# Second layer's temporaries packed by lifetime, expert pieces loaded into each slot as it comes free, a 17th slot, and the norm weights applied after the turn

## The reference

```python
for l in range(2):
    z = rms_norm(h, norm1_g[l]) @ w_in[l]
    y = concat(mlstm(..), mla(..), gla(..), conformer_conv(..))
    h = h + group_rms_norm(y, fuse_g[l], 4) @ w_out[l]
    u = rms_norm(h, norm2_g[l])            # h * rstd * norm2_g
    if l == 0: f = (silu(u @ w_gate) * (u @ w_up)) @ w_down     # dense, 2816 wide
    else:      f = moe_ffn(u, ...)         # 8 experts, each 1024 -> 2816 -> 1024
    h = h + f                              # moe: top 2 of 8 by u @ router, softmax of the two
return rms_norm(h, final_norm_g)
```

## Time and profile before

| | |
|---|---|
| median of 3 runs | 1104.01 us (1103.98 to 1105.52) |
| the profiled execution, its own time | 1104.98 us |
| its span, first to last instruction | 1103.1 us |
| granted TensorE clock | 0.998 of full |
| PE busy | 96% of the span |
| DVE, ACT, POOL busy | 28%, 28%, 23% |
| moved by DMA | 358.5 MB, mean 325 GB/s |
| first matmul of job 0 | at 430.58 us |
| expert jobs | 430.58 to about 1092 us |

### The profile page before, as it was taken

One profiled execution on the slowest core, in us unless ns is written; L12 is line 12 of the kernel. 1 busy time (PEld: TensorE's weight loads), 2 busy tenths in 40 slices (PEclk: granted clock), 3 DMA queues, 4 the chain that ended last, 5 costly groups with the idle time before them and its releaser, 6 DMA issues.

```text
span 1103.1 us, 27114 instructions
## 1 busy us (share of the span) xinstructions
PE 1063.6 (96%) x12186; PEld 766.0 (69%) x12186; DVE 305.1 (28%) x572; ACT 308.0 (28%) x571; POOL 251.0 (23%) x332
## 2 busy tenths in 40 slices
PE   7999999999999999999999999999989999999875
PEld 7888888888899887665656666766636766766531
DVE  4785644444558756110000010010000010010012
ACT  7868644434486871000000000000000000000011
POOL 9986300000078755400201002002001002001000
PEclk9999999999999999999999999999999999999999
DMA  9642995535424449999999999999999999999993
GB/s 302 208 158 78 391 351 188 169 139 151 134 68 167 163 167 419 411 417 390 416 420 416 419 418 417 419 419 418 418 421 417 419 419 419 419 419 419 420 418 156
DMA packets 81623, 358.50 MB, mean 325 GB/s; under 512 B 10108, under 2 KB 24654, under 8 KB 47840
## 3 DMA queue, kind: packets, MB, share of 16 engines
q1 hardware_dynamic: 76480, 344.15, 78.7%
q0 software_dynamic: 4848, 12.30, 3.2%
q10 hardware_dynamic: 176, 0.27, 0.1%
HBM read 350.35 MB, written 7.47 MB: 324 GB/s over the span
## 4 chain that ended last, share of the span: by engine, by line
PE 80%; DMA 8%; SPq 5%; ACT 3%; DVE 3%; issue 1%; DVEq 0%
PE bank L2718 25%; PE bank L2763 13%; PE bank L2730 5%; SPq L711 5%; PE bank L2194 4%; PE bank L2195 4%; PE bank L2196 4%; DMA ring<-in_moe_w_up_dram 3%; DMA low_raw<-in_moe_w_gate_dram 3%; DMA ring<-in_moe_w_down_dram 2%; PE bank L2770 2%; PE bank L2311 2%; PE bank L2313 2%; PE bank L2212 2%; PE bank L2213 2%; PE bank L2214 2%
## 5 line engine op out<-in xcount | busy, mean ns | idle before, releaser
L2718 PE MATMUL bank<-ring,spare 128*32 128x256 f32 x3028 | 181.1, 380 | 1.1 <-DMA ring<-in_moe_w_gate_dram 0.6
L2718 PEld LDWEIGHTS bank<-ring,spare 128*32 128x32 f32 x3028 | 120.2, 110 | 48.4 <-issue 8.3
L1057 ACT ACTIVATE high<-ring 128x2048 fp32r<-128x2048 f32 (+2 forms) x62 | 117.0, 1892 | 68.2 <-PE bank L2196 41.8
L830 POOL TENSOR_TENSOR low<-ring,high 128x512 fp32r<-128x512 f32 (+1 forms) x67 | 85.6, 1308 | 197.1 <-ACT high L1057 195.8
L1029 POOL DMA_INDIRECT expert_rows<-yrows,result_idx x15 | 15.1, 1004 | 397.0 <-ACT yrows L1428 394.0
L1525 DVE TENSOR_TENSOR low<-ring,high 128x2048 fp32r<-128x2048 f32 (+2 forms) x38 | 85.7, 2258 | 54.6 <-ACT high L1057 52.1
L2056 DVE TENSOR_TENSOR act_out<-bank,act_out 128x512 f32<-128x512 f32 (+3 forms) x37 | 20.5, 579 | 263.7 <-PE bank L2718 220.0
L2730 PE MATMUL bank<-ring,spare 128*64 128x256 f32 x700 | 86.4, 381 | 6.0 <-DMA ring<-in_moe_w_up_dram 6.0
L2763 PE MATMUL bank<-ring,hidT 128*32 128x256 f32 x1584 | 87.4, 379 | 0.0
L1446 ACT ACTIVATE hidT<-bank 128x512 f32<-128x512 f32 (+2 forms) x34 | 16.0, 536 | 231.9 <-PE bank L2743 231.9
L2044 DVE STREAM_TRANSPOSE spare<-back 128x768 f32<-128x768 f32 (+1 forms) x7 | 6.0, 861 | 250.9 <-DMA back<-token_rows,quad_idx 250.9
(11 more groups left out here) (478 smaller groups left out, 1772.4 us busy)
## 6 DMA issues: line engine op xcount, KB each, us to landing
ring<-in_moe_w_up_dram SPq DMA_DIRECT2D x72, 1024.0 KB, 27.6
ring<-in_moe_w_gate_dram SPq DMA_DIRECT2D x58, 1024.0 KB, 22.4
ring<-in_moe_w_down_dram SPq DMA_DIRECT2D x53, 1024.0 KB, 27.0
low_raw<-in_moe_w_down_dram SPq DMA_DIRECT2D x23, 1024.0 KB
ring<-in_w_in_dram SPq DMA_DIRECT2D x36, 512.0 KB, 5.7
raw_slots<-in_moe_w_gate_dram SPq DMA_DIRECT2D x15, 1024.0 KB
low_raw<-in_moe_w_gate_dram SPq DMA_DIRECT2D x15, 1024.0 KB
ring<-in_ffn_w_up_dram SPq DMA_DIRECT2D x22, 512.0 KB, 5.1
```

The lines of the kernel that those rows point to most:

```text
L830: last = pool.tensor_tensor(low[:, n % SPLIT, at], slot(n)[:, at], high[:, n % SPLIT, at].bitcast(F32), ALU.subtract)
L1057: act.activation(high[:, n % SPLIT, 0:width], slot(n)[:, 0:width], ACT.Copy).then_inc(s["high_ready"], 1)
L2718: last = pe.matmul(bank[b][32 * c:32 * c + 32, at:at + SEG], x[:, k, 32 * r:32 * r + 32], part, start=first and at == 0, stop=final and at ...
```

## The change

1. The second layer's temporaries in slots 5 to 10 are declared in an order by lifetime, so that they fill slots 5 to 8 only; short-lived ones share space (`gS`, `osq` over `qT`, `kT`; `dec`, `cqT` over `qtok`, `ktok`; `qksg` over `cumf` to `negm`; `probT` over `ckvT`, `rin`, `rt`). Eleven small tiles get space of their own. Slots 9 and 10 hold none.
2. `MOE_SLOTS` is reordered, and a slot that lay under temporaries waits for its own last readers (`SLOT_FREED`) and no longer for `mixers_done(1)`.
3. `un`, free after the attention's probabilities are turned, becomes a 17th slot `un_slot`: `DEEP = 17`, with piece 3 as its first.
4. `moe_g` and POOL's multiplication (L949) are gone. A small tile `gains` (feature p*8+k at partition p, column k) is loaded in layer 0 by one more DMA on POOL. PE reads h itself for L2653, with a step of 8 elements; POOL's L964 too. The norm weight is applied per partition when the turned tokens leave: for job 0 by four ACT activations with a scale and one DVE multiplication by a broadcast tile in place of two copies; for jobs 1 to 7 by one more DVE multiplication in place after the transpose.
5. `yrows` and `back` move over `u32`; job 0's tokens and the last squares go to `spare`.

```diff
-MOE_SLOTS = [4, 0, 1, 2, 3, 6, 7, 8, 9, 10, 5]
+MOE_SLOTS = [9, 10, 4, 5, 0, 8, 7, 1, 6, 2, 3]
-MOE_EARLY = 5
-DEEP = 16
+DEEP = 17
-RING_PLACE = [0, 1, 2, 3, 4, 5, 6, 7, 8, 9, 14, 15, 11, 12, 13, 10]
+RING_PLACE = [0, 1, 2, 16, 3, 4, 5, 6, 7, 8, 9, 14, 15, 10, 11, 12, 13]
+UN_AT = RING_PLACE.index(DEEP - 1)
+OVER_PLACES = [v for v in range(DEEP) if v != UN_AT][:RING]
@@ temporaries
             sb("ring_0_to_4", [P, 5, PIECE], F32, part)
-            (ckvT, cqT, moe_g, qtok, ktok, rin, rt, dec, gS, vm, gE, cumf, ... in a row)
+            with ExitStack() as first:
+                ckvT, rin, rt
+            probT, vm
+            with ExitStack() as scores:
+                qT, kT
+            gS, osq
+            with ExitStack() as tokens:
+                qtok, ktok
+            dec, cqT, gE, junk
+            with ExitStack() as gates:
+                cumf, aj, mrun, negm
+            qksg
@@ slots of the expert stage
+ [un_slot[:, :]]
+        SLOT_FREED = {5: (("pv_ready", DEPTH),),
+                      8: (("ga_ready", HEADS * DEPTH), ("qk_ready", DEPTH)),
+                      7: (("num_ready", DEPTH), ("y_c", DEPTH)),
+                      6: (("go_ready", DEPTH), ("y_g", DEPTH))}
@@ SP, expert()
                     elif RING_PLACE[g] < RING:
-                        if g == MOE_EARLY:
-                            sp.wait_ge(*mixers_done(1))
-                        elif MOE_SLOTS[RING_PLACE[g]] == 5:
-                            sp.wait_ge(s["hg_ready"], 2 * TT)
+                        for freed, count in SLOT_FREED.get(MOE_SLOTS[RING_PLACE[g]], ()):
+                            sp.wait_ge(s[freed], count)
                         sp.wait_ge(s["low_ready"], BEFORE_OF[MOE0 + RING_PLACE[g]] + 1)
                     elif RING_PLACE[g] < RING + SPLIT:
                         sp.wait_ge(s["piece_used"], MOE0 - SPLIT + RING_PLACE[g] - RING + 1)
-                    else:
-                        sp.wait_ge(*mixers_done(1))
+                    elif RING_PLACE[g] < RING + SPLIT + 2:
+                        sp.wait_ge(*mixers_done(1))
+                    else:
+                        sp.wait_ge(s["p_tr"], 3 * DEPTH)
@@ POOL
+                    pool.dma_start(gains[:, :], norm2_g[DEPTH - 1].rearrange("(p k) -> p k", p=P)).then_inc(s["moe_in"], 16)   # layer 0
-                if l:
-                    pool.wait_ge(s["qT_tr"], 4)
-                    pool.wait_ge(s["kT_tr"], 4)
-                    pool.dma_start(moe_g[:, :], bc(norm2_g[DEPTH - 1:DEPTH, :], [P, D])).then_inc(s["moe_in"], 16)
-            for t in range(TT):
-                for i in range(2):
-                    pool.wait_ge(s["h_ready"], 8 + 2 * t + i + 1)
-                    (un half t, i = h half * moe_g half, permuted).then_inc(s["hg_ready"], 1)
-                pool.wait_ge(s["hg_ready"], 2 * t + 2)
+                pool.wait_ge(s["h_ready"], 8 + 2 * t + 2)
-                feats = un[:, t, :].rearrange("p (b k q c) -> p b q k c", b=2, k=4, q=4)
+                feats = h[:, t, :].rearrange("p (q c b k) -> p b q k c", q=4, c=32, b=2)
@@ ACT
+            def x_out(x, n):
+                for k in range(4):
+                    last = act.activation(x[:, k, 0:n], bank[5][:, k * n:(k + 1) * n], ACT.Copy, scale=gains[:, k:k + 1])
+                last.then_inc(s["x_act"], 1)
@@ DVE
-                dve.transpose(x_of(n)..., xrows_q...).then_inc(s["xT_tr"], 1)
+                x = x_of(n)[:, :, 0:32 * r]
+                chain.done(dve.transpose(x..., xrows_q...))
+                chain.wait()
+                dve.tensor_tensor(x, x, bc(gains[:, :].unsqueeze(2), [P, KD, 32 * r]), ALU.mult).then_inc(s["xT_tr"], 1)
+            def x_out(x, n):
+                dve.tensor_tensor(x[:, 4:8, 0:n], bank[6][:, 0:4 * n].rearrange("p (k n) -> p k n", k=4),
+                                  bc(gains[:, 4:8].unsqueeze(2), [P, 4, n]), ALU.mult).then_inc(s["x_dve"], 1)
@@ PE
-            pe.wait_ge(s["hg_ready"], 2 * TT)
+            pe.wait_ge(s["h_ready"], 12)
+            by_k = h[:, :, :].rearrange("q t (p k) -> q t k p", k=KD)
-                        last = pe.matmul(bank[b][...], un[:, t, kd * P:(kd + 1) * P], sel[:, t, 0:96], ...)
+                        last = pe.matmul(bank[b][...], by_k[:, t, kd, :], sel[:, t, 0:96], ...)
```

More of the change, by code:

```diff
@@ L210, in build @@
             sb("ring_0_to_4", [P, 5, PIECE], F32, part)
[L211 to L222, removed]
-            vm = sb("vm", [P, TT, 256], F32, part)
[L224 to L241, removed]
+            with ExitStack() as first:
+                ckvT = sb("ckvT", [P, S], F32, first)
+                rin = sb("rin", [P, TT, 5, 32], F32, first)
+                rt = sb("rt", [P, 4, TT, 5, 16], F32, first)
+            probT = sb("probT", [P, 3, 4, P], F32, part)
+            vm = sb("vm", [P, TT, 256], F32, part)
             with ExitStack() as scores:
@@ L244, in build @@
                 kT = sb("kT", [96, 4, S], F32, scores)
-            probT = sb("probT", [P, 3, 4, P], F32, part)
+            gS = sb("gS", [P, 4, 3, P], F32, part)
             osq = sb("osq", [P, TT, 4, 64], F32, part)
+            with ExitStack() as tokens:
+                qtok = sb("qtok", [P, TT, 4, 96], F32, tokens)
+                ktok = sb("ktok", [P, TT, 4, 96], F32, tokens)
+            dec = sb("dec", [P, 4, 384], F32, part)
+            cqT = sb("cqT", [P, 2, S], F32, part)
+            ctok = cqT[:, :, :]
+            gE = sb("gE", [P, 5, P], F32, part)
+            junk = sb("junk", [P, 256], F32, part)
+            with ExitStack() as gates:
+                cumf = sb("cumf", [4, S], F32, gates)
+                aj = sb("aj", [4, S], F32, gates)
+                mrun = sb("mrun", [4, S], F32, gates)
+                negm = sb("negm", [P, S], F32R, gates)
+            qksg = sb("qksg", [P, 4, S], F32, part)
         with ExitStack() as part:
@@ L283, in build @@
         router = sb("router", [P, KD, E])
+        gains = sb("gains", [P, KD])
+        gref = sb("gref", [P, 2, 2])
+        smax = sb("smax", [P, TT, 4])
+        psums = sb("psums", [P, TT, 4])
+        mcol = sb("mcol", [P, 16])
+        mden = sb("mden", [P, TT, 4])
+        gss = sb("gss", [P, TT, 4])
+        gls = sb("gls", [P, TT, 4])
+        grd = sb("grd", [P, TT, 4])
+        bst = sb("bst", [P, TT, 6])
+        bag = sb("bag", [P, TT, 2])
         invf = sb("invf", [P, 16])
@@ L335, in build @@
         with ExitStack() as part:
-            yrows = sb("yrows", [P, D], F32, part)
-            back = sb("back", [P, D], F32, part)
-            xrows = back
+            over_x = sb("over_x", [P, TT, D], F32, part)
         with ExitStack() as part:
-            over_x = sb("over_x", [P, TT, D], F32, part)
+            un_slot = sb("un_slot", [P, PIECE], F32, part)
         keep_un = ctx.enter_context(nc.sbuf_tensor("keep_un", [P, TT, D], F32))
@@ L392, in build @@
         with ExitStack() as part:
+            with ExitStack() as rows:
+                yrows = sb("yrows", [P, D], F32, rows)
+                back = sb("back", [P, D], F32, rows)
+                xrows = back
             u32 = sb("u32", [P, KD, S], F32, part)
@@ L1108, in normalize_group @@
                     chain.wait()
-                    chain.done(act.activation(junk[:, :], y[:, t, g * 256:(g + 1) * 256],
+                    chain.done(act.activation(zl[:, 0, 0:256], y[:, t, g * 256:(g + 1) * 256],
                                               ACT.Square, accum_out=ss[:, t, g:g + 1]))
@@ L1475, in half @@
                     act.wait_ge(s["xT_tr"], j)
-                    act.activation(x_of(j)[:, 0:4, :], bank[5][:, :].rearrange("p (k n) -> p k n", k=4), ACT.Copy).then_inc(s["x_act"], 1)
+                    x_out(x_of(j), P)
                     own_slots(j, bank[OWN_BANK][:, 2 * P:2 * P + 1])
@@ L2652, in _ @@
                     for t in range(TT):
-                        last = pe.matmul(bank[b][:, k * 96:(k + 1) * 96], un[:, t, kd * P:(kd + 1) * P], sel[:, t, 0:96],
+                        last = pe.matmul(bank[b][:, k * 96:(k + 1) * 96], by_k[:, t, kd, :], sel[:, t, 0:96],
                                          start=(t == 0), stop=(t == TT - 1))
```

31 lines of the change are left out of this document (14 added, 17 removed).

## The result

| | before | after |
|---|---|---|
| median, us | 1104.11 (1103.98 to 1105.52) | 1113.43 (4 runs, 1112.04 to 1113.89) |
| profiled execution, us | 1104.98 | 1113.34 |
| its span, us | 1103.1 | 1111.5 |
| granted clock | 0.998 | 0.991 |

The ratio is 1.0081, interval 1.0069 to 1.0093: 9.3 us slower, where 1101.5 was forecast, in a range that ended at 1104.4. Two executions of all that follow lie far off and stand in no median or ratio: one of e10's four (3377.68 us) and one of the kernel before beside e11 to e14 (1216.83).

What follows compares the result with a forecast made beforehand. The prediction took the end to be the 264th piece's landing plus a fixed tail. Only the 17th slot counted, all other terms 0: 1104.0 - 2.5 = 1101.5 us, range 1099.3 to 1104.4.

Steps and rivals of the forecast that it cites:

- Step 1: First pieces loaded earlier, before job 0: gain 0, upper bound 1.4 us, since slots hold the stream back anyway.
- rival B: Start of job 0: its stall goes too, with a quiet DMA queue, and job 0 takes 90.9; 1099.6 us, chance 0.11.
- Step 2: 17th slot at half job 1's start: the stream is one piece further, so the end moves by -2.5 us.
- Rival C: Stream after job 0: the transfer was hidden anyway, so no piece is gained; 1104.0 us, chance 0.06.
- Step 3, the product: L2653 before job 0: PE reading h as weights with a 32-byte step costs 0, bounds 0 and +2.1 us.
- rival A: Product before job 0: the strided weight load costs +2.1 us and eats the slot; 1103.6 us, chance 0.27.
- D: Rival on L2653's pace: slower records lose the slot; a threefold pace gives +7.6 - 2.5, 1109 us, chance 0.06.
- Step 3, DVE beside POOL: Routing before job 0: POOL's multiplication going away frees nothing and could ease DVE; 0, bounds -0.5 to +0.5 us.
- Step 3, the copies: Behind the product: ACT's four scaled operations and DVE's multiplication replace two copies at +0.
- Step 4: Later jobs: DVE's added multiplication, about 1.0 us per job behind the transpose, is hidden; +0, without cover 7 us.
- Step 5: Layer 0: one more small DMA on POOL costs 0, bounds 0 and +0.6 us.
- The signs: Trace marks named beforehand, among them 17 loads by 419 us; wrong if gain above 4 us or jobs 1 to 7 change over a microsecond.

Runs made afterwards that it cites:

- e10: Kernel before, but POOL's four scalings read h with the 32-byte step, norm weights left out of jobs 1 to 7; ratio 1.0050.
- e11: e14 with 16 slots in place of 17, early loads kept; 1105.83 us, ratio 1.0015.
- e14: Changed kernel, but POOL copies h into the space of act_out, and PE and POOL's scalings read that copy contiguously; 1103.15 us, ratio 0.9990.
- e15: The kernel before, unchanged, run once more with a profile; 1104.08 us, its profile 1103.79.
- e9: As e7, but PE reads h with a step of 2 elements (8 bytes); one execution, 1104.33 us.
- e7: Kernel before, but PE's product for job 0 reads h as weights with a 32-byte step, without norm weights there; 1111.86 us, ratio 1.0069.
- e1: Changed kernel, but POOL's scalings read h in its own order, without the step (table's features wrongly ordered); 1107.06 us, ratio 1.0029.
- e2: Changed kernel, but POOL's scalings wait for sel_ready, so none runs beside DVE's routing; 1106.03 us, ratio 1.0019.
- e3: Changed kernel with 20 filler products in place of 4 before the second rank product, keeping PE busy; 1109.90 us, ratio 1.0055.
- e13: e14 with 16 slots and late loads (piece 5 and later wait for the last transposes); 1105.69 us, ratio 1.0013.
- e16: e14 without DVE's multiplication of the turned tokens, norm weights left out of jobs 1 to 7; 1102.78 us, ratio 0.9988.
- e8: As e7, but PE reads h with a step of 4 elements (16 bytes); one execution, 1109.77 us.
- e12: e14 with late loads: piece 5 and later wait for the last transposes, 17 slots kept; 1102.74 us, ratio 0.9985.
- e5: e2 with late loads: piece 5 and later wait for the last transposes, on another chip; 1108.28 us, ratio 1.0044.

## Why the prediction was wrong

Measured against e15, an execution near the median of before (the one the prediction rests on had job 0 0.8 us later), the changed kernel's profile goes as follows: the product starts 4.2 us late and takes 3.95 longer, job 0 takes 2.7 longer, the slot takes back 2.7, the rest adds about 1.4. The profiles differ by 9.55.

- **What bounds the kernel now**: right. The end is a landing plus a tail. Between two late down pieces the distance is 2.46 as before (1093.99 and 1096.45, rows below), and what the start of job 0 and job 0 lost stood at the end, less the slot: against the first profile of before 10.07 us at job 1's start and 8.34 at the end of the span.

```profile
1093.99 1.94 PE L2786 MATMUL bank<-ring,hidT 128*64 128x512 f32 x8 [0.53 <-DMA ring<-in_moe_w_down_dram]
1096.45 3.65 PE L2786 MATMUL bank<-ring,hidT 128*64 128x512 f32 x16 [0.52 <-DMA ring<-in_moe_w_down_dram]
```

- **Step 1, early loads, 0**: right (e11 to e14). The quiet queue gave job 0 nothing: rival B fell.
- **Step 2, the 17th slot, -2.5**: right; 2.46, 2.7 and 2.95 in three pairs. Rival C fell.
- **Step 3, the product, 0 with bounds 0 and +2.1**: the step that failed. It measured +4.1 (7.9 against 3.8). The row of PE's moving operand, on which the 0 stood, was of the wrong operand and the wrong step: at 8 bytes the weights are nearly free too (e9), and the kernel has 32. POOL's row pointed the right way, but a ratio of one engine (+56%) was no upper bound for another (+108%). The prediction cited the Trainium skill's rule of 16-byte lines for rival A and gave it 0.27; applied to the step, two accesses a line against one, it says on which side of the edge 8 and 32 bytes lie.
- **Step 3, what stands behind the product**: taken as nothing, without a term. Rivals A and D priced the slow records alone; D, which had the mechanism, comes to +4.1 - 2.5 = 1.6 us for 247 ns. None had the clock. PE held back by its own weight loads was given half clock from within the product (e7, e1, e2, e3). In e7 4.5 us of it lie in job 0, whose first 64 records took 5.83 us against 3.66 in e15: 2.2 of the 2.8 us by which job 0 is longer. The earlier trace rows show a whole clock in every stage, and I took it for granted. In the changed kernel the clock fell earlier, in the gap that DVE left, and 4.6 us of half clock lie in job 0.
- **Step 3, DVE beside POOL, taken 0 within -0.5 and +0.5**: wrong; the product starts 2.5 us late in e10's trace and 4.2 in the changed kernel. There `idf` and `oh` of the two tiles make 3.5 us more than in e15, and PE's small products in front of the product, at half clock after the gap, 1.0 more. I read L949 as something that goes away, but its reading with a step of 32 bytes moved into L963, later and beside more of DVE's chain. The one slow `oh` (0.64) did not price that: it ran from 421.55, when L949 had ended (421.48) and the first contiguous scaling ran, and e1, where no scaling steps, has it at 0.58 too. The Trainium skill ("SBUF — State Buffer", section "Who interferes with whom") has DVE and GpSimd share a pair of ports that one instruction holds until it ends, for DVE's casts in its two-port modes and for its operations with two inputs in SBUF. The trace agrees in part: beside strided scalings `idf` and `oh` took 2.01 and 1.93. But the first tile's `oh` (421.65, 0.17) ran inside a strided scaling (420.41 to 422.47), and the one of e1 (420.80, 0.17) inside a contiguous one (419.80 to 421.37), without a delay. POOL's times are rough, so what DVE waits for in POOL's operation stays open.
- **Step 3, the copies, 0**: right: 4.63 us from the product's start to job 0 in e13 as in e15.
- **Step 4, later jobs, 0**: the multiplication takes 0.69 behind the transpose of job 3 (697.93, next work at 740.28) and is hidden. e16 leaves 0.2 to 0.4 us that can't be told from nothing.
- **Step 5 and the new order of the temporaries, 0**: not separated. All that is neither slot, loads nor stride costs 1.5 us (e13), which no step had.
- **The signs**: the 17 loads by 419 us, piece 49 issued at job 0's end (533.02 against 532.89) and the 2.46 us between late pieces came as named. That jobs 1 to 6 change by more than a microsecond in sum was named as a sign of being wrong; they did, by -2.2 us, but most of that is step 2 itself, job 4 waiting 2 us less.

## What to carry to other kernels

Before an operand is read with a step in place of a copy, ask which operand of which engine it is and how many of its elements share 16 bytes: as PE's weights, fp32 with a step of 16 or 32 bytes took 1.7 times as long to load and twice as long a record here, and with one of 8 bytes hardly longer. When a prediction says that an operation goes away, follow its access pattern to the operation that takes it over, and look what runs beside that one. Where a slow product stood at the start of a stage that PE sets, it was paid twice here, once in the product and once in the clock that it left to what follows.

## What the runs showed of the hardware

- The clock fell to half while PE was busy without a gap: in e7 from 428.33, 3.0 us after the strided product began, and in e3 5.9 us after, for 10.2 and 6.8 us. In the profiles of the contiguous forms it stayed whole there, but for e12's. Being busy alone did not keep it: with weight loads of 335 and 329 ns (e7, e8) it fell, with 196 and 192 (e9, e15) it did not.
- PE's records of a strided product have the same pace at either clock (7.75 us at half in the changed kernel, 7.9 mostly at whole in e3), while the contiguous one took 7.04 us at half and 3.8 at whole.
- Jobs 2 and 3 took 89.9 to 90.0 us in the traces of one chip and 90.7 to 91.3 in those of the others, half job 1 58.8 on all, and the kernel before as long on each (1103.8 to 1104.2). Why before isn't shorter on the first, though PE sets its job 0, no trace shows. Comparing variants across chips most likely misled: late loads looked 2.2 us worse (e5 against e2, on two chips) and are 0.4 us better on one (e12 against e14).
